# The normalisation behind the operand work, in the last stage of a Hyena and pooling encoder layer

## The reference

```python
u = h * (1.0 + scale) + shift                     # adaLN, scale/shift/gate from silu(c) @ w_ada + b_ada
proj = u @ w_in + b_in                            # 1024 -> 3072
hy_streams, hy_gate, pool_in, pool_gate = split(proj)
y_h = hyena_branch(hy_streams, ...)               # short conv, two long bidirectional convolutions by FFT, gates
y_p = pool_branch(pool_in, pool_w, pool_scale)    # window means 2/4/8/16 minus token, a matrix per group
y = concat([y_h * silu(hy_gate), y_p * silu(pool_gate)], -1)
out = gate * (y @ w_out + b_out)
return layer_norm(ALPHA * x + out) * ln_g + ln_b   # over the 1024 channels of each token
```

## Time and profile before

| | before |
|---|---|
| time, median of 3 runs | 1180.67 us (1175.66 to 1180.91) |
| profiled execution: time, span | 1175.66 us, 1173.8 us |
| PE busy, PEld busy | 1088.2 us (93%), 840.9 us (72%) |
| DVE busy | 850.9 us (72%) |
| ACT busy | 584.4 us (50%) |
| granted TensorE clock, mean | 0.972 |
| the last stage's loop | about 967 to 1171 us of the span |

### The profile page before, as it was taken

The page is one execution under the profiler, slowest core; times in us unless marked ns, Lnnn a source line. Parts: engine busy times, 40 slices in busy tenths (PEclk is TensorE's granted clock), DMA queues, the critical chain, the costliest instruction groups (busy, mean ns, idle before and its releaser), DMA issues. The chain is left out here.

```text
span 1173.8 us, 14214 instructions
## 1 busy us (share of the span) xinstructions
PE 1088.2 (93%) x4928; PEld 840.9 (72%) x4928; DVE 850.9 (72%) x1081; ACT 584.4 (50%) x769; POOL 12.5 (1%) x32
## 2 busy tenths in 40 slices
PE   3799789999999999998999999898999779999996
PEld 1278668888888877766888877666788557888885
DVE  6699985555455545649999746554999957989887
ACT  4068864434545444537777635444888753222210
POOL 0001000000000000000000000000000000000000
PEclk8789999999999999999999999999999879999998
DMA  9999855677675435688999568778899999476531
GB/s 341 346 311 288 281 180 167 204 246 236 235 251 171 173 108 196 213 263 225 299 282 285 172 210 263 263 232 252 248 286 297 276 313 324 130 218 185 180 108 54
DMA packets 155132, 273.24 MB, mean 233 GB/s; under 512 B 11503, under 2 KB 49519, under 8 KB 153396
## 3 DMA queue, kind: packets, MB, share of 16 engines
q1 hardware_dynamic: 151605, 266.74, 71.4%
q0 software_dynamic: 3168, 5.51, 2.1%
q10 hardware_dynamic: 288, 0.08, 0.0%
HBM read 178.95 MB, written 98.57 MB: 236 GB/s over the span
## 5 line engine op out<-in xcount | busy, mean ns | idle before, releaser
L177 PE MATMUL u_pp<-uh_uhi,prj_whi 128*128 128x512 f32 x768 | 309.7, 403 | 14.2 <-DVE u_ulo L741 8.7
L179 PE MATMUL u_pp<-uh_uhi,prj_wlo 128*128 128x512 f32 x768 | 305.1, 397 | 0.0
L178 PE MATMUL u_pp<-u_ulo,prj_whi 128*128 128x512 f32 x768 | 304.7, 397 | 0.0
L177 PEld LDWEIGHTS u_pp<-uh_uhi,prj_whi 128*128 128x128 f32 x768 | 145.8, 190 | 57.0 <-issue 14.8
L179 PEld LDWEIGHTS u_pp<-uh_uhi,prj_wlo 128*128 128x128 f32 x768 | 145.7, 190 | 34.4
L178 PEld LDWEIGHTS u_pp<-u_ulo,prj_whi 128*128 128x128 f32 x768 | 146.1, 190 | 32.2
L1282 DVE TENSOR_TENSOR p_alo<-xin_pair,p_ahi 128x1024 fp32r<-128x1024 f32 x32 | 39.2, 1226 | 97.3 <-ACT p_ahi L1219 97.3
L1219 ACT ACTIVATE p_ahi<-xin_pair 128x1024 fp32r<-128x1024 f32 x32 | 33.9, 1060 | 124.0 <-PE p_ps L179 117.0
L593 ACT ACTIVATE fs_khi<-fs_k 128x1024 fp32r<-128x1024 f32 x32 | 34.0, 1062 | 42.2 <-DVE fs_k L570 42.2
L554 PE MATMUL fs_s<-fs_khi,flt_tab 64*128 64x512 f32 x256 | 50.6, 417 | 2.5 <-ACT prj_row L598 2.5
L177 PE MATMUL p_first<-uh_uhi,prj_whi 128*128 128x512 f32 x128 | 51.1, 399 | 1.6 <-DVE prj_wlo L2270 1.6
(11 more groups left out here) (212 smaller groups left out, 2112.0 us busy)
## 6 DMA issues: line engine op xcount, KB each, us to landing
xin_pair<-kseq SPq DMA_DIRECT2D x32, 512.0 KB, 4.3
kfreq<-xin_pair SPq DMA_DIRECT2D x32, 512.0 KB, 5.1
xseq<-p_xo SPq DMA_DIRECT2D x32, 512.0 KB, 7.7
p_k_re<-kfreq SPq DMA_DIRECT2D x64, 256.0 KB, 5.7
p_k_im<-kfreq SPq DMA_DIRECT2D x64, 256.0 KB, 4.9
bseq<-p_out SPq DMA_DIRECT2D x32, 512.0 KB, 5.1
prj_ws<-in_t_win SPq DMA_DIRECT2D x24, 512.0 KB
kseq<-prj_row SPq DMA_DIRECT2D x22, 512.0 KB, 4.1
```

Of the source, the lines that this page charges most:

```text
L177: nc.tensor.matmul(out, w[0], m[0], start=start, stop=False, skip_group_check=True)
L178: nc.tensor.matmul(out, w[0], m[1], start=False, stop=False, skip_group_check=True)
L179: return nc.tensor.matmul(out, w[1], m[0], start=False, stop=stop, skip_group_check=True)
```

## The change

`norm` moves from the first to the last place in VectorE's step, and `root` from the middle to the last place in ScalarE's. No instruction is added or removed, and TensorE's, SyncE's and GpSimd's programs are as they were.

```diff
@@ def scalar(act), the loop over step in range(0, GS + 1)
                 evac(step + 1)
             if step + 3 < GS:
                 high(step + 3)
-            if step >= 1:
-                root(step - 1)
             if step + 2 < GS:
                 pooled_high(step + 2)
             if step + 1 < GS:
                 conv_high(step + 1)
+            if step >= 1:
+                root(step - 1)
@@ def vector(dve), the loop over step in range(0, GS + 1)
-            if step >= 1:
-                norm(step - 1)
             if step + 1 < GS:
                 gated_rows(step + 1)
@@
                 conv_low(step + 1)
             if step < GS:
                 skip(step)
+            if step >= 1:
+                norm(step - 1)
```

## The result

| | before | after |
|---|---|---|
| time, median (range) | 1180.91 us (1175.66 to 1184.54), 7 runs | 1189.87 us (1187.11 to 1190.78), 7 runs |
| ratio | | 1.0069, 95% interval 1.0053 to 1.0087 |
| profiled execution: span | 1173.8 us | 1185.8 us |
| PE busy, DVE busy | 1088.2, 850.9 us | 1093.3, 851.3 us |

The changed kernel is 0.7% slower. Of the 12.0 us between the two spans not all belongs to the edit: the first matmul of product(0), which lies ahead of everything that was moved, starts at 974.25 us instead of 969.36. So the stretches are compared inside the last stage, from one transposition to the next.

What follows compares the result with a forecast made beforehand. TensorE was taken to set the pace, with VectorE bounding the end; 2.9 + 1.3 + 4.9 = 9.1 us (8.3 to 10.0) on the median of 1180.67 us gave 1189.8 us, +0.8%, range 1182 to 1195.

Steps and rivals of the forecast that it cites:

- The end, 4.9 us: Behind the last transposes: norm(13) becomes the third norm left there on VectorE, so norm(15) ends the kernel 4.90 us later.
- The first norm, 2.9 us: Step 1: norm(0) comes behind low(4), which waits for high(4) and its DMA; pooled(2) starts late, 2.93 us in all.
- The steps, 1.3 us: Steps 2 to 12: the loop through transposes, VectorE and pooled takes 13.03 to 13.19 against 12.99 us, 0.12 each.
- The first handover: In each step's loop, from TensorE's transposes to VectorE: between 0 and 0.16 us.
- Root on ScalarE and the DMA queue, zero: In the steps: root ahead of evac still leaves z ready 3 us early, and SyncE's order is unchanged; cost zero.
- The gain: Rival, 0.02: operands made first remove TensorE's waits for low(1), conv_low(0) and evac(2), 4.44 us together, giving 1176.2 us.
- the first rival: Chance 0.12: TensorE hides its part at the start and in the steps; only the end's 4.9 us stay, 1185.6 us.
- More waits in the steps: Rival, 0.11: VectorE has no slack, so late DMAs or longer steps add about 2 us; about 1192 us.
- The falling clock: Rival, 0.05: behind the 2.8 us gap at pooled(2) the clock falls to 1.2 GHz, losing 2.5 us; 1192.3 us.

Runs made afterwards that it cites:

- the two operations of norm(13): Changed kernel, but norm's first two operations (L2304, L2306) stand first in VectorE's step, its rest last, norm(15) whole; 1.0021 of before.
- 0.60 us more: Changed kernel with one more VectorE operation of 0.60 us ahead of norm in steps 1 to 12: 1.0120; kernel before with the same: 1.0016.

## Why the prediction was right

The result, 1189.87 us, is on the forecast of 1189.8 to 0.1 us, and that agreement is luck. The direction, the two mechanisms and the largest term were right. In the stage the change costs 6.0 us, below the forecast's sum of 9.1 and below its bounds of 8.3 to 10.0. The other 3 us of the 8.96 us between the medians show in none of the stretches that the edit touches.

- **The end, 4.9 us: right.** 32.02 and 32.07 us against 27.26 and 27.27 is 4.8. The row of three norms was there nearly to the hundredth (19.47 for 19.50), and the experiments that took work from behind the last transposes shortened it: by 2.6 us with the two operations of norm(13), by all of it with the old order from step 8.
- **The first norm, 2.9 us: right place, wrong size.** TensorE waited at pooled(2) for L2306, as forecast, but step 1 grew by 1.0 us in both profiles of the changed kernel. The term came from one execution of the kernel before. There low(4) could have begun 981.86 - 977.71 = 4.15 us behind the transposes of unit 2; in the changed kernel's profile it began 985.96 - 983.71 = 2.25 us behind them. Of these 1.9 us, 1.1 is TensorE being later: step 0 took 9.46 us instead of 8.35, by the low clock in product(0). The other 0.8 is the arrival of x(4), with high(4) 10.61 us behind product(0)'s start instead of 11.38. With the clock full the growth was 15.31 - 13.03 = 2.3 us, nearer to the forecast, and once 4.4 us, with the clock falling in the step itself. The chain was also read too narrowly: not the arrival of x(4) alone makes norm(0) late, as its earlier load showed.
- **The steps, 1.3 us: too much.** It was 0.2 to 0.3, and TensorE's timeline has no wait in steps 2 to 13, where the forecast had a short one in most. The loop was put at 13.03 to 13.19 us; the 0.60 us more put it at 12.98. It was worked out with 1.25 us from skip to norm, and that row holds a handover from the skip to its own norm, which the new order doesn't have: 1.14 us. Against that, the handover from L2306 to pooled was taken as 0.06 us, from another pair of operations, and was 0.15. The first handover, left open between 0 and 0.16, was 0.03 (1010.61 - 1009.98 - 0.60). That the cover was just used up was right.
- **Root on ScalarE and the DMA queue, zero: right.** root(1) ran at 1006.50 and evac(4) directly behind it, well ahead of its transposes at 1010.70; no wait of these is among TensorE's in steps 2 to 13.
- **The sum.** From step 1 to the end it is 202.09 - 196.09 = 6.0 us, and 6.0 again in the second pair of profiles. The times say 0.69% and 0.90%, or 8 and 11 us, with lower ends of 6.3 and 8.6. The kernel before shows 1.8 us against itself. The rest is not explained. What lies ahead of step 1 has the same program in both and differs between executions: product(0) started at 974.3 and 973.5 in the changed kernel, 969.4 and 977.4 in the one before. One rival stays open: step 0 was long, by the low clock, in six of the ten profiles with a changed order somewhere and in none of the three with the old order throughout. That would be worth up to 1.6 us, and three profiles are too few to tell it from chance.
- **The rivals.** The gain was not there: of the three waits ahead of the first norm, those for conv_low(0) and evac(2) stayed (1.82 and 0.69 us), and that for low(1) was missing in both profiles of the changed kernel, but there again with the old order in step 1 (1.01 us) and with 0.60 us more (1.79 us), so the order doesn't decide it. TensorE hid its part in the steps nearly whole, as the first rival had it, but not at the first norm. More waits in the steps showed once, for 0.3 us (x(4) loaded earlier). The falling clock, to which I gave 0.05, did not happen to the changed kernel at this gap, but it did in an experiment (in the last section).

No order tried here beats the kernel before: none of the edited kernels had a stage under its 196.1 us.

## What to carry to other kernels

When one engine is full, the other's free time is worth only as much as it lies on the right side of a wait: moving the operation that frees a buffer behind work that waits for the full engine closes a loop through both, though each has the same work as before. And in a pipeline over units, count what each engine still has to do behind the last thing that the full engine hands over; moving finished work later by one unit costs next to nothing in the middle (0.2 to 0.3 us in twelve steps here), and is paid at the end (4.8 us). A start-to-start time read from a row belongs to its neighbours: if they change, check whether it held a handover. And a term that rests on one DMA's arrival in one execution is worth a range, not a number: this one came out between 1.0 and 4.4 us.

## What the runs showed of the hardware

TensorE's clock fell around waits of 1.4 to 2.8 us in some executions and not in others. Stretches of the kernel with the old order from step 13 (bounds, length; PE, PEld, DVE, ACT, POOL busy; granted clock, DMA share, GB/s):

```profile
985.00:987.00 2.00, 2.00 (x11) 1.59 (x10) 2.00 (x4) 1.31 (x2) 0.00 (x0) 1.00 1.13 330
987.00:990.00 3.00, 0.57 (x3) 0.13 (x1) 2.94 (x3) 0.00 (x0) 0.00 (x0) 1.00 1.19 292
990.00:993.00 3.00, 2.88 (x7) 2.28 (x8) 2.88 (x6) 0.78 (x2) 0.00 (x0) 0.56 1.15 310
993.00:996.00 3.00, 3.00 (x13) 2.41 (x12) 1.94 (x5) 0.95 (x1) 0.00 (x0) 0.87 1.04 401
```

Its pooled(2) came after this gap:

```profile
990.12 0.56 PE L177 MATMUL p_first<-uh_uhi,prj_whi 128*128 128x512 f32 x1 [2.55 <-DVE p_y L2308]
990.48 0.63 PE L178 MATMUL p_first<-uh_uhi,prj_whi 128*128 128x512 f32 x1
```

After 2.55 us without a matmul the granted clock goes down to the 1.2 GHz level and the matmuls stand 0.42 us apart for about 3 us, so the gap cost its own time and 1.6 us more. With the old order from step 14 a gap of 2.01 us at the same place left the clock at 1.00:

```profile
991.00:994.00 3.00, 3.00 (x13) 2.48 (x14) 2.89 (x6) 0.78 (x2) 0.00 (x0) 1.00 1.14 314
```

That is the rival of the falling clock, at 1.6 us instead of the 2.5 that it had in the prediction. The Trainium skill, TensorE: Matmul & The Clock Gate, section HAM oscillation, says that a wait between bursts of matmuls makes the next burst start at the lower clock. The rows agree with it behind the 2.55 us, and not behind the 2.01 us.

The clock also makes the two lengths of step 0, one and the same code. From product(0)'s start to the transposes of unit 2 the granted clock is 1.00 in all seven profiles in which step 0 takes 7.9 to 8.4 us, 0.82 in the five with 9.4 to 9.5, and 0.72 in the one with 10.53. In the changed kernel:

```profile
975.00:977.00 2.00, 2.00 (x7) 1.52 (x6) 1.23 (x2) 0.00 (x0) 0.00 (x0) 0.50 1.03 409
```

product(0) stands behind a wait of 1.35 to 2.8 us for conv_low(0) in all thirteen. How long that wait was doesn't tell the two apart (2.63 us and a short step in one, 1.46 us and a long one in another, 1.46 and a short one in a third); what decides stays open.
